# The first gather of the experts' tokens, ordered part by part and split around half of the first gate

## The chip, the core and the metric

The kernel runs on one core of a Trainium2 chip. Five engines work from instruction streams of their own and meet through semaphores: TensorE (PE, matrix products; its weight loads are listed apart as PEld), VectorE (DVE), ScalarE (ACT), GpSimd (POOL) and SyncE (SP), which here issues nearly all DMAs. The metric is the device time of one execution in microseconds (us), as the median of several runs.

## What is computed

One decoder block over 272 tokens of width 1024 (16 meta tokens and 256 real ones): a pooling mixer and a gated delta rule side by side, an output projection, and then a mixture of 32 experts in 4 groups. Only the last part matters here:

```
u = rmsnorm(h, norm_ffn_w)
p_grp, g_idx = top_k(softmax(u @ w_grp + b_grp), 1)            # one of 4 groups
w_e, e_idx   = top_k(softmax(expert logits of that group), 2)  # two of its 8 experts
for each expert e:                                             # 32 of them
    hdn = silu(u @ w_gate[e]) * (u @ w_up[e])                  # 1024 -> 512
    y  += (comb[:, e] * hdn) @ w_down[e]                       # 512 -> 1024
out = rmsnorm(h + y, norm_final_w)[:, 16:]
```

The weights of an expert are three arrays of 2 MiB in float32, 201 MB for all 32, and each is read once.

## The kernel before

**The experts' stage.** An expert computes at most 64 tokens (`SLOTS`). A matrix `hot` (token x slot, one or zero) picks them: the product of x, held as a rounded part `xhi` and a remainder `xlo` (both in the format of fast products), with `hot` gathers the tokens of four experts at once, transposed, 256 columns wide. The tokens come in two tiles of 128 (`TT` = 2, index t), the width 1024 in eight k tiles of 128 rows (`KT`), two of which make a *part* (`PARTS` = 4). A gathered part stands in a PSUM bank, from which a copy that multiplies by the norm's gain takes it to `xgT` (in the trace a piece of `bench`).

**The first gather** (`gather_first`, L2155 to L2184) has a bank for each part (`FIRST_BANK`, L2163): parts 0 to 3 in banks 5, 4, 7 and 6. It runs the products of `xhi` for parts 0 to 2, tile by tile, then those of `xlo` for parts 0 to 2, and then part 3 with both. ScalarE takes parts 0 and 2 to `xgT` (L1118, semaphore `xgT_side`), VectorE parts 1 and 3 (`bring`, L1723, semaphore `xgT`), all on `gathered`. VectorE makes `hot` (L1662) and then the remainders (`lows`, L1668): first the columns of parts 0 to 2 for both tiles, then those of part 3.

**Gate, up and down.** `gate_up` (L2218) multiplies the 64 slots of an expert by its gate and then its up weights, eight k tiles each, two products in a tile (two for each one in the trace, since these are float32). The first gate waits on `xgT_side` ahead of k tiles 0 and 4 and on `xgT` ahead of 2 and 6. It writes bank 5, where part 0 had stood. Behind it stand two products that count the tokens of the experts (`count_all`, L2110 and L2111), then up, then two parts of the next gather (L2142), then down (L2276).

**The stream of weights.** SyncE fills a ring of nine slots of 2 MiB and a spare half slot. Load n is array n % 3 (gate, up, down) of expert n // 3. Loads 9 to 18 come in two halves each (L743), shifted by half a slot: the first half of load 9 goes to the spare half, its second half into the first half of slot 0, the first half of load 10 into the second half of slot 0, and so on. The second half of load 9 is issued when gate 0 has read k tiles 0 to 3 (semaphore `half`), the first half of load 10 when gate 0 is done (`gate`), and so on with up and down. SyncE issues in this order and waits for each in turn.

**VectorE behind the first gather**: `bring(0, 1)`, `bring(0, 3)`, `weigh` (what the exponentials on ScalarE need), `weighed` (the weights of the two experts of each token, L1688 to L1694), `settle` (the largest count, L1699), and then `slots_of(1)`, which makes `hot` of the next four experts (L1710).

## Time and profile before

| | |
|---|---|
| median of 3 runs | 772.37 us (772.29 to 773.62) |
| profiled execution | 772.13 us |
| its span, first to last instruction | 770.4 us |
| PE busy | 750.6 us (97%) |
| DVE / ACT / POOL busy | 323.0 / 311.6 / 124.9 us |
| DMA | 240.56 MB, mean 312 GB/s |
| chain that ended last | PE 83%, DMA 11%, DVE 3%, issue 2%, ACT 1% |

Times in the rows are from the start of the span. The experts' stage begins at 318 and fills the rest. A time of an engine that waits is only a loss if what waits for that engine is late; so the profile is read by stage, and each wait by who comes last. Durations overlap on one engine (an instruction is listed until its result is written, the next starts before that), so what a piece occupies is read from the starts of two in a row.

### The profile page before, as it was taken

Reading aid. Unit: us, or ns where it says so; the run is one execution under the profiler, and the core shown is the slowest. Engines: PE = TensorE matmul, PEld = TensorE weight load, DVE = VectorE, ACT = ScalarE, POOL = GpSimd, SP = SyncE. Lnnn points to the kernel's source line nnn. Section 1 sums busy time; section 2 is a strip of 40 time slices with the busy share of each in tenths; the row PEclk is TensorE's granted clock in tenths of the full one; section 3 lists DMA queues with packets and bytes.
Section 4 is the critical chain, followed back from the end, with each engine's and each line's share of the span. In section 5 each row is a group of like instructions: output and inputs, shape, how many; then the busy total and the mean of one; then the engine's idle time right before and its main releaser. Section 6 shows DMA issues by size and latency. Waiting matters only on the chain.

```text
span 770.4 us, 16167 instructions
## 1 busy us (share of the span) xinstructions
PE 750.6 (97%) x6544; PEld 538.9 (70%) x6544; DVE 323.0 (42%) x795; ACT 311.6 (40%) x632; POOL 124.9 (16%) x209
## 2 busy tenths in 40 slices
PE   8999999999999999999999999999999999998995
PEld 8989989998999988755555555565555555455552
DVE  4895787678675855712211311221222113012112
ACT  6976678576684744712112121222112121111123
POOL 7473242225423640000000000000000000000000
PEclk9999999999999999999999999999999999999999
DMA  8537554554754479999999999999999999999993
GB/s 206 148 86 194 149 145 131 138 151 111 191 140 125 153 241 327 374 407 421 427 424 430 426 428 427 429 424 428 425 428 427 427 429 424 430 426 428 422 415 127
DMA packets 83265, 240.56 MB, mean 312 GB/s; under 512 B 7281, under 2 KB 65762, under 8 KB 69746
## 3 DMA queue, kind: packets, MB, share of 16 engines
q1 hardware_dynamic: 82882, 238.67, 81.4%
q8 instruction: 55, 0.90, 0.5%
q10 hardware_dynamic: 304, 0.79, 0.4%
q14 instruction: 24, 0.20, 0.1%
HBM read 238.40 MB, written 1.05 MB: 311 GB/s over the span
## 4 chain that ended last, share of the span: by engine, by line
PE 83%; DMA 11%; DVE 3%; issue 2%; ACT 1%; SPq 0%; DVEq 0%
PE banks L2218 24%; PE banks L1863 22%; PE banks L2276 12%; DMA ring<-in_expert_w_up_dram 10%; PE banks L2142 3%; PE banks L2231 3%; PE banks L2060 3%; PE banks L1983 1%; PE banks L1996 1%; PE banks L2252 1%; PE banks L2044 1%; PE banks L2000 1%; PE banks L1987 1%; DMA room<-in_w_in_dram 1%; PE banks L2021 1%
## 5 line engine op out<-in xcount | busy, mean ns | idle before, releaser
L2218 PE MATMUL banks<-ring,bench 128*64 128x256 f32 x2016 | 235.6, 388 | 5.1 <-DMA ring<-in_expert_w_up_dram 3.6
L2218 PEld LDWEIGHTS banks<-ring,bench 128*64 128x64 f32 x2016 | 144.5, 134 | 102.6 <-issue 19.5
L1863 PE MATMUL banks<-rounded 128*128 128x256 f32 (+2 forms) x1320 | 193.5, 293 | 0.4 <-DVE room L1481 0.4
L1863 PEld LDWEIGHTS banks<-rounded 128*128 128x128 f32 x1320 | 168.0, 188 | 3.7 <-issue 0.6
L1762 DVE TENSOR_TENSOR bench<-banks,bench 128x256 f32<-128x256 f32 x32 | 13.6, 424 | 254.3 <-PE banks L2218 182.7
L2276 PE MATMUL banks<-ring,bench 128*64 128x512 f32 x512 | 116.9, 598 | 0.3 <-ACT bench L1144 0.3
L1155 ACT ACTIVATE ysb<-banks 64x512 f32<-64x512 f32 x63 | 37.3, 592 | 150.3 <-PE banks L2276 149.5
L2276 PEld LDWEIGHTS banks<-ring,bench 128*64 128x64 f32 x512 | 33.9, 136 | 62.8 <-issue 60.2
L923 ACT ACTIVATE rounded<-room 128x1024 fp32r<-128x1024 f32 x64 | 67.4, 1054 | 22.1 <-PE banks L1863 15.0
L1144 ACT ACTIVATE bench<-banks 128x256 f32<-128x256 f32 x32 | 12.3, 385 | 142.8 <-PE banks L2252 142.8
L1381 DVE TENSOR_TENSOR rounded<-room,rounded 128x1024 fp32r<-128x1024 f32 x49 | 62.4, 1273 | 15.2 <-ACT rounded L923 14.2
L1250 POOL TENSOR_TENSOR rounded<-room,rounded 128x256 fp32r<-128x256 f32 x60 | 44.1, 767 | 60.7 <-ACT rounded L923 60.7
L1732 DVE SCALAR_TENSOR_TENSOR ylo<-ysb,bench,yhi 128x512 fp32r<-128x512 f32 x30 | 21.2, 749 | 64.6 <-ACT yhi L1162 64.6
L1432 DVE SCALAR_TENSOR_TENSOR desk<-banks,prmT,desk 128x271 f32<-128x271 f32 (+5 forms) x72 | 35.3, 490 | 4.6 <-ACT desk L933 2.5
L1139 ACT ACTIVATE bench<-banks 128x256 f32<-128x256 f32 x32 | 12.3, 384 | 57.1 <-PE banks L2218 57.1
L2142 PE MATMUL banks<-hot,xhi 128*128 128x256 f32 x112 | 34.6, 332 | 0.0
L1723 DVE TENSOR_TENSOR bench<-banks,gain 128x512 f32<-128x512 f32 x30 | 20.8, 692 | 20.8 <-PE banks L2142 18.7
L2142 PEld LDWEIGHTS banks<-hot,xhi 128*128 128x128 f32 x112 | 21.1, 188 | 11.2 <-issue 11.2
L2142 PE MATMUL banks<-hot,xlo 128*128 128x256 f32 x112 | 28.8, 280 | 0.0
L2231 PE MATMUL banks<-yhi,give 128*128 128x512 f32 x60 | 23.7, 396 | 0.0
L2231 PE MATMUL banks<-ylo,give 128*128 128x512 f32 x60 | 23.5, 391 | 0.0
L2142 PEld LDWEIGHTS banks<-hot,xlo 128*128 128x128 f32 x112 | 21.3, 191 | 0.2 <-issue 0.2
(317 smaller groups left out, 876.4 us busy)
## 6 DMA issues: line engine op xcount, KB each, us to landing
ring<-in_expert_w_down_dram SPq DMA_DIRECT2D x27, 2048.0 KB, 24.8
ring<-in_expert_w_up_dram SPq DMA_DIRECT2D x25, 2048.0 KB, 26.9
ring<-in_expert_w_gate_dram SPq DMA_DIRECT2D x24, 2048.0 KB, 25.9
room<-in_w_in_dram SPq DMA_DIRECT2D x56, 512.0 KB, 4.0
ring<-in_expert_w_gate_dram SPq DMA_DIRECT2D x10, 1024.0 KB, 9.8
ring<-in_expert_w_up_dram SPq DMA_DIRECT2D x8, 1024.0 KB, 10.4
ring<-in_expert_w_up_dram SPq DMA_DIRECT2D x12, 512.0 KB, 6.5
ring<-in_expert_w_down_dram SPq DMA_DIRECT2D x6, 1024.0 KB, 8.7
```

The lines of the kernel that those rows point to most:

```text
L923: nc.scalar.activation(whi[:, n % HI_SLOTS], win[:, n % WIN_SLOTS].rearrange("p k c -> p (k c)"), ACT.Copy).then_inc(S("whi"), 1)
L1155: nc.scalar.activation(ysb[g * SLOTS:(g + 1) * SLOTS, half * 512:(half + 1) * 512], pb[7][half * 64:half * 64 + SLOTS, :], ACT.Copy).then_ ...
L1250: ins = nc.gpsimd.tensor_tensor(wlo[:, lo_slot(n), cols], w[:, cols], whi[:, n % HI_SLOTS, cols].bitcast(F32), ALU.subtract)
L1381: V.tensor_tensor(wlo[:, lo_slot(n)], w, whi[:, n % HI_SLOTS].bitcast(F32), ALU.subtract).then_inc(S("wlo"), 1)
L1432: ins = V.scalar_tensor_tensor(acc[:, i, f + sh:L], p[:, 0:L - f - sh], prmT[:, tap * 24 + col:tap * 24 + col + 1], acc[:, i, f + sh:L], A ...
L1732: V.scalar_tensor_tensor(ylo[:, cols], ysb[:, cols], wslot[:, 0:1], yhi[:, cols].bitcast(F32), ALU.mult, ALU.subtract).then_inc(S("ylo"), 1)
L1863: ins = T.matmul(o, a, b[:, k, lo_at:L], start=(k == 0 and n == 0), stop=(k == KT - 1 and n == 2))
L2060: ins = T.matmul(pb[2 * i + half], a[:, i * P:(i + 1) * P], w[:, half * 512:(half + 1) * 512], start=(kk == 0 and first), stop=(kk == KT - ...
L2142: ins = T.matmul(pb[4][:, k * WIDE:(k + 1) * WIDE], x[:, t, ch:ch + P], hot[:, t, :], start=(t == 0 and x is xhi), stop=(t == TT - 1 and x ...
L2218: ins = T.matmul(pb[5 + c][half * 64:half * 64 + SLOTS, 0:256], xgT[:, q % ROOMS, kt, j * SLOTS:(j + 1) * SLOTS], ws[kt // 4][:, kt % 4, h ...
L2231: ins = T.matmul(pb[2 * t + half], give[:, t * P:(t + 1) * P], y[:, half * 512:(half + 1) * 512], start=False, stop=True, skip_group_check ...
L2276: ins = T.matmul(pb[7][half * 64:half * 64 + SLOTS, :], hT[:, j % 2, j // 2 * SLOTS:(j // 2 + 1) * SLOTS], ws[j // 2][:, j % 2, half * 512 ...
```

## The change

The first gather goes part by part, each with its remainders: parts 0 and 1 ahead of gate 0, then k tiles 0 to 3 of gate 0, then parts 2 and 3, then k tiles 4 to 7. VectorE makes the remainders in eight pieces of 256 columns in the same order, those of part 3 behind `bring(0, 1)`, and `weigh` stands ahead of `bring(0, 3)`. ScalarE's and SyncE's instructions stay as they are.

```diff
--- before.py
+++ after.py
@@ -1672,9 +1672,13 @@
             pick(1)
             first_slots(0)
             first_slots(1)
-            for cols in (slice(0, 3 * D // PARTS), slice(3 * D // PARTS, D)):
+            def part_lows(part):
+
                 for i in range(TT):
-                    lows(i, cols)
+                    lows(i, slice(part * D // PARTS, (part + 1) * D // PARTS))
+
+            for part in range(PARTS - 1):
+                part_lows(part)
 
             def weigh():
 
@@ -1744,8 +1748,9 @@
                 else:
                     dve.wait_ge(S("kept"), 1)
                     bring(0, 1)
+                    part_lows(PARTS - 1)
+                    weigh()
                     bring(0, 3)
-                    weigh()
                     weighed()
                     settle()
                 for e in range(EXPERTS):
@@ -2152,35 +2157,27 @@
                                        ident[:, n * 64:(n + 1) * 64], start=True, stop=True, skip_group_check=True)
                     ins.then_inc(S("gathered"), 1)
 
-                def gather_first():
-
-                    per = KT // PARTS
-
-                    def products(x, part, t):
-
-                        for k in range(per):
-                            ch = (part * per + k) * P
-                            ins = T.matmul(pb[FIRST_BANK[part]][:, k * WIDE:(k + 1) * WIDE], x[:, t, ch:ch + P], hot[:, t, :],
-                                           start=(k == 0 and t == 0 and x is xhi), stop=(t == TT - 1 and x is xlo), skip_group_check=True)
-                        return ins
-
-                    for t in range(TT):
-                        pe.wait_ge(S("hot"), t + 1)
-                        pe.wait_ge(S("xhi"), t + 1)
-                        for part in range(PARTS - 1):
+                per = KT // PARTS
+
+                def products(x, part, t):
+
+                    for k in range(per):
+                        ch = (part * per + k) * P
+                        ins = T.matmul(pb[FIRST_BANK[part]][:, k * WIDE:(k + 1) * WIDE], x[:, t, ch:ch + P], hot[:, t, :],
+                                       start=(k == 0 and t == 0 and x is xhi), stop=(t == TT - 1 and x is xlo), skip_group_check=True)
+                    return ins
+
+                def gather_parts(some):
+
+                    for part in some:
+                        for t in range(TT):
+                            pe.wait_ge(S("hot"), t + 1)
+                            pe.wait_ge(S("xhi"), t + 1)
                             products(xhi, part, t)
-                    for t in range(TT):
-                        pe.wait_ge(S("xlo"), t + 1)
-                        for part in range(PARTS - 1):
+                        for t in range(TT):
+                            pe.wait_ge(S("xlo"), TT * part + t + 1)
                             ins = products(xlo, part, t)
-                            if t == TT - 1:
-                                ins.then_inc(S("gathered"), 1)
-                    for t in range(TT):
-                        products(xhi, PARTS - 1, t)
-                    for t in range(TT):
-                        pe.wait_ge(S("xlo"), TT + t + 1)
-                        ins = products(xlo, PARTS - 1, t)
-                    ins.then_inc(S("gathered"), 1)
+                        ins.then_inc(S("gathered"), 1)
 
                 def landed(e, c):
 
@@ -2208,6 +2205,8 @@
                             pe.wait_ge(S("give"), pairs + i)
                     ws = [half_at(3 * e + c, n, again).rearrange("p (k q h j) -> p k h q j", k=KT // 2, h=2, j=2) for n in range(2)]
                     for kt in range(KT):
+                        if first and c == 0 and kt == KT // 2:
+                            gather_parts(range(PARTS // 2, PARTS))
                         if first and c == 0 and kt % 4 == 0:
                             pe.wait_ge(S("xgT_side"), kt // 4 * 2 + 2)
                         if first and c == 0 and kt % 4 == 2:
@@ -2284,7 +2283,7 @@
                         for k in range(KT // PARTS):
                             gather(0, part, k)
                 else:
-                    gather_first()
+                    gather_parts(range(PARTS // 2))
                 for e in range(EXPERTS):
                     q, j, i, g = e // 4, e % 4, e // 2, e % 2
                     gate_up(e, 0, "gate")
```

On TensorE, at the start of the experts' stage, before. The rows give the line, the operation, out<-in and how many in a row; L2163 is the first gather, L2218 gate 0 and then up 0, L2110 and L2111 the counting:

```order
L2106 MATMUL banks<-ticks,give 128x32
L2163 MATMUL banks<-hot,xhi 128x256 x12
L2163 MATMUL banks<-hot,xlo 128x256 x12
L2163 MATMUL banks<-hot,xhi 128x256 x4
L2163 MATMUL banks<-hot,xlo 128x256 x4
L2218 MATMUL banks<-ring,bench 64x256 x16
L2110 MATMUL banks<-ticks,give 128x32
L2111 MATMUL banks<-ticks,give 128x32
L2218 MATMUL banks<-ring,bench 64x256 x16
```

The same place now; the gather is L2166 and the gate L2217:

```order
L2111 MATMUL banks<-ticks,give 128x32
L2166 MATMUL banks<-hot,xhi 128x256 x4
L2166 MATMUL banks<-hot,xlo 128x256 x4
L2166 MATMUL banks<-hot,xhi 128x256 x4
L2166 MATMUL banks<-hot,xlo 128x256 x4
L2217 MATMUL banks<-ring,bench 64x256 x8
L2166 MATMUL banks<-hot,xhi 128x256 x4
L2166 MATMUL banks<-hot,xlo 128x256 x4
L2166 MATMUL banks<-hot,xhi 128x256 x4
L2166 MATMUL banks<-hot,xlo 128x256 x4
L2217 MATMUL banks<-ring,bench 64x256 x8
L2115 MATMUL banks<-ticks,give 128x32
```

Gate 0 is cut in two, and the sixteen products of parts 2 and 3 stand in the cut.

On VectorE, from the second `hot` on, before; L1668 are the remainders, L1723 the brings, L1681 and L1683 `weigh`, and from L1688 on `weighed`:

```order
L1662 TENSOR_TENSOR hot<-iota_c,bench 128x256
L1668 SCALAR_TENSOR_TENSOR xlo<-late,rs,xhi 128x768 x2
L1668 SCALAR_TENSOR_TENSOR xlo<-late,rs,xhi 128x256 x2
L1723 TENSOR_TENSOR bench<-banks,gain 128x512 x2
L1681 TENSOR_SCALAR rs<-bench 128x1 x2
L1683 TENSOR_TENSOR rs<-bench 128x1 x2
L1688 RECIPROCAL rs<-rs 128x1 x2
```

The same place now, with L1727 the brings and L1685 and L1687 `weigh`:

```order
L1662 TENSOR_TENSOR hot<-iota_c,bench 128x256
L1668 SCALAR_TENSOR_TENSOR xlo<-late,rs,xhi 128x256 x6
L1727 TENSOR_TENSOR bench<-banks,gain 128x512
L1668 SCALAR_TENSOR_TENSOR xlo<-late,rs,xhi 128x256 x2
L1685 TENSOR_SCALAR rs<-bench 128x1 x2
L1687 TENSOR_TENSOR rs<-bench 128x1 x2
L1727 TENSOR_TENSOR bench<-banks,gain 128x512
L1692 RECIPROCAL rs<-rs 128x1 x2
```

The two brings are apart now: one behind six pieces of the remainders, the other behind the last two and `weigh`, and everything from L1692 on behind it.

## Rows read from the trace of the kernel before

**Rows 1.** Windows: each engine's busy us (x instructions), PE clock, DMA share, GB/s.

```profile
345.00:445.00 100.00, 100.00 (x705) 57.38 (x705) 21.71 (x51) 20.01 (x39) 0.00 (x0) 1.00 1.01 426
```

**Rows 2.** Chain that ended last: start us, us, what; gate and up of two experts, then loads.

```profile
430.15 7.26 PE banks L2218 x64
...
456.87 7.26 PE banks L2218 x64
...
611.91 36.88 DMA ring<-in_expert_w_up_dram
```

**Rows 3.** Windows around the gap in the DMA engines' work; columns as in Rows 1.

```profile
324.50:327.00 2.50, 2.50 (x24) 1.46 (x22) 1.95 (x14) 1.90 (x5) 0.00 (x0) 1.00 0.64 164
...
329.00:333.00 4.00, 4.00 (x30) 2.39 (x28) 2.01 (x6) 0.39 (x1) 0.00 (x0) 1.00 1.00 354
```

**Rows 4.** Timeline of SyncE's DMA issues: start us, us, line, operation, out<-in, count.

```profile
315.37 0.33 SPq L743 DMA_DIRECT2D spare<-in_expert_w_gate_dram  x1
324.84 0.33 SPq L743 DMA_DIRECT2D ring<-in_expert_w_gate_dram  x1
326.65 2.62 SPq L743 DMA_DIRECT2D ring<-in_expert_w_up_dram  x2
330.75 3.78 SPq L743 DMA_DIRECT2D ring<-in_expert_w_down_dram  x2
```

**Rows 5.** DMA issues, windows 324.5:325.5 and 326.3:327.5: kind, count, KB each, us to landing.

```profile
ring<-in_expert_w_gate_dram SPq DMA_DIRECT2D x1, 1024.0 KB, 4.8
...
ring<-in_expert_w_up_dram SPq DMA_DIRECT2D x1, 1024.0 KB, 6.4
```

**Rows 6.** Timeline of PE, 316 to 331; [idle before <-releaser].

```profile
318.47 1.70 PE L2163 MATMUL banks<-hot,xhi 128*128 128x256 f32 x12 [0.31 <-DVE hot L1662]
320.00 1.88 PE L2163 MATMUL banks<-hot,xlo 128*128 128x256 f32 x12
321.72 0.64 PE L2163 MATMUL banks<-hot,xhi 128*128 128x256 f32 x4
...
322.76 3.85 PE L2218 MATMUL banks<-ring,bench 128*64 128x256 f32 x32
326.54 0.28 PE L2110 MATMUL banks<-ticks,give 128*128 128x32 f32 x1
...
330.64 0.39 PE L2142 MATMUL banks<-hot,xhi 128*128 128x256 f32 x1
```

**Rows 7.** Timeline of DVE, windows of 314 to 334, some cut between two remainders.

```profile
318.57 0.43 DVE L1662 TENSOR_TENSOR hot<-iota_c,bench 128x256 fp32r<-128x256 f32 x1
...
318.91 1.01 DVE L1668 SCALAR_TENSOR_TENSOR xlo<-late,rs,xhi 128x768 fp32r<-128x768 f32 x1
...
319.85 1.41 DVE L1668 SCALAR_TENSOR_TENSOR xlo<-late,rs,xhi 128x768 fp32r<-128x768 f32 x2
...
320.77 0.87 DVE L1668 SCALAR_TENSOR_TENSOR xlo<-late,rs,xhi 128x256 fp32r<-128x256 f32 x2
...
321.17 0.48 DVE L1668 SCALAR_TENSOR_TENSOR xlo<-late,rs,xhi 128x256 fp32r<-128x256 f32 x1
...
321.76 0.69 DVE L1723 TENSOR_TENSOR bench<-banks,gain 128x512 f32<-128x512 f32 x1
...
324.80 0.23 DVE L1688 RECIPROCAL rs<-rs 128x1 f32<-128x1 f32 x2 [0.85 <-ACT rs L1125]
...
327.34 0.75 DVE L1710 TENSOR_TENSOR hot<-iota_c,bench 128x256 fp32r<-128x256 f32 x2
```

**Rows 8.** Timeline of PEld (weight loads), 314 to 334.

```profile
320.91 0.77 PEld L2163 LDWEIGHTS banks<-hot,xlo 128*128 128x128 f32 x6 [0.16 <-DVE xlo L1668]
```

**Rows 9.** Timeline of ACT around 321.5: the copies of parts 0 and 2.

```profile
321.51 0.48 ACT L1118 ACTIVATE bench<-banks,gain 128x256 f32<-128x256 f32 x1 [2.11 <-PE banks L2163]
...
321.88 1.20 ACT L1118 ACTIVATE bench<-banks,gain 128x256 f32<-128x256 f32 x3
```

## The prediction

> **What bounds the kernel now.** I read the profile from its end backwards. First the stretch 345 to 445: the 16 DMA engines are busy all the time, at 426 GB/s [rows 1], and TensorE is busy too, so the reader has to ask which of the two is ahead. The chain of waits answers. Two experts take TensorE 456.87 - 430.15 = 26.72 us [rows 2] and use six loads of 2.097 MB, 12.58 MB; the stream needs 12.58 MB / 426 GB/s = 29.5 us for them. TensorE is thus faster by 2.8 us in each pair, frees ring slots sooner than they can be filled, and the queue of loads grows, until a load issued at 611.91 takes 36.88 us to land and TensorE starts to wait for weights [rows 2]. The end of the kernel is therefore set by the stream of weights. A delay of TensorE at 320 us costs nothing by itself (over the ten pairs up to 611.91 TensorE gains some 28 us on the stream); it costs what it leaves the DMA engines **without work**.
>
> That makes one hole the thing to look at. From 324.5 to 327.0 the DMA engines are busy 0.64 of the time and move 164 GB/s [rows 3]: idle 0.36 x 2.5 = 0.90 us, and short of 426 GB/s by 0.66 MB, 1.54 us of the stream. It is there because SyncE may issue the next half load only once gate 0 has read the first half of its weights (issue at 324.84), and the one behind it once gate 0 is done (326.65); the load before these was issued at 315.37 [rows 4]. A half load is 1.049 MB, 2.46 us of the stream. The one of 324.84 landed after 4.8 us [rows 5], so 4.8 - 2.46 = 2.34 us pass besides the transfer.
>
> **The part that changes, before.** TensorE starts the first gather at 318.47, gate 0 at 322.76, and is done with gate 0 at 326.54, where the counting products stand [rows 6]. These are 32 products of the gather and 32 of the gate (two in the trace for each one in the code). 16 of the gate take (326.54 - 322.76) / 2 = 1.89 us, 0.118 us each, and at that pace 64 make 7.55 us; the stretch took 8.07, so the stalls in it are 0.52 us.
>
> **What the change does to VectorE.** No product is added. The remainders are eight instructions of 256 columns for two of 768 and two of 256. From the starts 318.91 and 319.85 a 768 piece occupies VectorE 0.94 us, from 320.77 and 321.17 a 256 piece 0.40 us [rows 7]. Six pieces ahead of the first bring are 2.40 us against 2 x 0.94 + 2 x 0.40 = 2.68 us before it; after that two follow it. They end 0.48 us after their start [rows 7]: at 319.39, 319.79, 320.19, 320.59, 320.99, 321.39.
>
> The Trainium skill, "VectorE: DVE Perf Modes", section "The TRN2 errata — SBUF-src ops pay a fixed extra latency per instruction", speaks against this split: the fixed cost is paid by each piece, and it wants 512 elements or more. The starts here bear out a fixed part of 0.40 - 256 x (0.54 / 512) = 0.13 us, 0.52 us for four more instructions; by the rule alone the change would lose that much if VectorE were the limit, and by the rows it is hidden, since the first piece is ready sooner.
>
> **TensorE through the first half.** It now starts with two products of part 0 for tile 0, 318.47 to 318.71. Tile 1's `hot` is ready at 318.57 + 0.43 = 319.00 [rows 7]; six products covered this wait, two do not. With 0.06 us from VectorE's end to TensorE (318.91 + 1.01 + 0.06 = 319.98, close to the 320.00 of the first remainder product), it goes on at 319.06 to 319.30, waits for the remainder of 319.39, runs 319.45 to 319.69, waits for that of 319.79, runs 319.85 to 320.09. Part 1 needs no waits that matter: 320.09 to 321.04 (its second remainder is ready at 320.65, and wanted at 320.80).
>
> Now gate 0 must wait for part 0's copy, which was hidden before behind the products of part 3. The pair that closed part 0 began at 320.91 [rows 8] and ScalarE started the copy at 321.51 [rows 9], 0.60 us later. So ScalarE starts at 319.85 + 0.60 = 320.45; its second copy started 0.37 us after the first and takes 0.48 [rows 9], ready at 321.30. Gate 0 starts at 321.36, a **new stall** of 0.32 us. Its k tiles 2 and 3 need VectorE's bring of part 1: that pair begins at 320.80, so the bring starts at 321.40, takes 0.69 [rows 7], and is ready at 322.09, where TensorE wants it at 321.36 + 0.94 = 322.30. Hidden, with 0.2 us to spare. The first half of gate 0 ends at 321.36 + 1.89 = 323.25.
>
> **Through the second half.** Parts 2 and 3 run 323.25 to 325.14; their remainders are long there. Part 2's closing pair begins at 323.96, ScalarE copies from 324.56, ready at 325.41, and TensorE goes on at 325.47: a **second stall** of 0.33 us. VectorE's bring of part 3 starts at 324.90 + 0.60 = 325.50 and is ready at 326.19, wanted at 326.41. Gate 0 ends at 325.47 + 1.89 = 327.36. Against 326.54 TensorE is **0.8 us later**. The rest of VectorE's queue moves with it: the weights of the experts (from 324.80 before) wait now behind the bring, start near 326.3, and the `hot` of 327.34 comes near 329.6 [rows 7]; the gather that wants it is at 330.64 + 0.8 [rows 6]. Hidden, by 1.5 us or more; if it were not, TensorE would stall by the difference.
>
> **What the stream gets.** The half of slot 0 is freed at 323.25 instead of 322.76 + 1.89 = 324.65; with the 0.19 us to the issue of 324.84, SyncE issues at 323.44, **1.40 us earlier**. The next issue is at 326.65 + 0.8 = 327.45, **later**, and so are all behind it. By landings: before 324.84 + 4.8 = 329.64, and the next could land by the later of 329.64 + 2.46 = 332.10 and 326.65 + 4.8 = 331.45, thus 332.10. After: 323.44 + 4.8 = 328.24, and the next by the later of 330.70 and 327.45 + 4.8 = 332.25. The hole is not closed, it is moved behind the early half load. The stream stands **0.15 us later** than before. The following half loads, 0.8 us later too, have slack: the one issued near 334.20 (the second of the two from 330.75 to 334.53 [rows 4]) could land at 335.0 + 4.8 = 339.8 and the stream is at 332.25 + 3 x 2.46 = 339.63, another 0.17 us at most. I take 0.15: the measured landing 326.65 + 6.4 = 333.05 [rows 5] is 0.95 behind the 332.10 of this sum, so that the queue really was fuller than the sum has it. The same row bounds the gain: with 0.95 us more in the queue before the later load the stream could come out 0.9 us earlier, the idle of the hole; the other end is the whole delay of TensorE, +0.8.
>
> The profiled execution took 772.13 us, its span 770.4. With +0.15 it is 772.28; it stands 0.24 under the median of 772.37, so I carry the difference to the median: **772.5 us**.
>
> **The rivals.**
> *TensorE's delay counts in full* (the queue is not the limit where I think): 772.37 + 0.8 = 773.2. For it: TensorE is 100 us of 100 busy [rows 1]. Against: the wait of 36.88 us for a load [rows 2].
> *The hole is closed*: the early half load fills it and the later one finds the queue still busy. 0.9 us of idle come back, 771.4. For it: the landing of 333.05; against: one half load holds 2.46 us, and 327.45 - 323.44 is 4.0.
> *The short pieces cost more*, the rule above: were pieces issued every 0.48 us, their full duration, the sixth would end at 321.79, bring 1 would be ready at 322.48, TensorE wanted it at 322.30; gate 0 ends 0.2 to 0.4 us later still, 772.8. The starts of 320.77 and 321.17 speak against it. The page named above is where it comes from.
> *Slower by over 0.2%*: TensorE stops before every pair of k tiles of gate 0, because each hand-over (product, copy, product: 0.60 + 0.85 us) is exposed in full. That is 4 x 1.45 = 5.8 less the 2 x 1.9 of cover that products of other parts give, some 2.0 us more, so 2.8 in all, and the hole takes it one for one beyond the 0.65 us of slack (332.10 - 331.45) : 774.5. It decides from a delay of 2.2 us on. The brings have 0.2 us to spare twice, which is what speaks for it; that all four are late by so much is unlikely.
> *Faster by over 0.2%*: all of the 1.54 us and the shortfall at 329 to 333 (426 - 354 GB/s over 4 us, 0.68 us [rows 3]) come back: 770.2.
>
> **How the numbers follow.** 0.2% is 1.54 us, about what a measurement can tell here from no change. Forecast 0.55; full delay 0.15; hole closed 0.17; short pieces 0.04; slower 0.06; faster 0.03. The first four lie within 0.2%: 0.91. For the range: down to the closed hole, 771.4; up past the full delay, 773.2, to 772.5 + 1.25 = 773.8, since one of the three runs shown lies 1.25 us above the median. Left outside: the two last rivals and little more.
>
> **What would show each step.** In the new profile: gate 0 starting near 321.4 with a short idle before it, counted from 318.47 of the first product; a second idle of 0.3 before its second half; the counting products near 327.4; the issues of SyncE at 323.4 and 327.5; and the low share of the DMA engines cut in two, one piece near 325 and one near 328.5. The forecast is wrong if the counting products come before 327.0 or after 328.5, if ScalarE or VectorE starts its copies more than 0.2 us off the times above, or if the DMA engines show one hole or none.

## The result: 1.4 us slower, and the profile after

| | before | after |
|---|---|---|
| median of 22 runs | 772.47 us | 773.99 us |
| ratio | | 1.0018 (95% interval 1.0012 to 1.0024) |
| profiled execution | 772.13 us, span 770.4 | 775.07 us, span 773.3 |
| first product of the gather | 318.47 | 319.70 (318.42 in a second trace) |

The change costs 1.4 us (0.9 to 1.9). The profiled executions are 2.9 apart; that the first product comes 1.2 us later in the first trace after is the spread of single executions, as the second trace of the same kernel shows. All that follows is therefore counted **from the first product of the gather**, which I call zero. Three executions of the experiments, which took 830 to 3821 us, are slow ones and count in no ratio.

TensorE after, from zero = 319.70 (against [rows 6]; L2166 is the gather, L2217 the gate and up, L2115 the counting):

```profile
319.70 1.09 PE L2166 MATMUL banks<-hot,xhi 128*128 128x256 f32 x4 [0.31 <-DVE hot L1662]
320.69 0.90 PE L2166 MATMUL banks<-hot,xlo 128*128 128x256 f32 x4
321.42 0.64 PE L2166 MATMUL banks<-hot,xhi 128*128 128x256 f32 x4
321.90 0.63 PE L2166 MATMUL banks<-hot,xlo 128*128 128x256 f32 x4
322.67 2.03 PE L2217 MATMUL banks<-ring,bench 128*64 128x256 f32 x16
324.63 0.73 PE L2166 MATMUL banks<-hot,xhi 128*128 128x256 f32 x4
325.20 0.62 PE L2166 MATMUL banks<-hot,xlo 128*128 128x256 f32 x4
325.65 0.64 PE L2166 MATMUL banks<-hot,xhi 128*128 128x256 f32 x4
326.13 0.63 PE L2166 MATMUL banks<-hot,xlo 128*128 128x256 f32 x4
326.75 2.03 PE L2217 MATMUL banks<-ring,bench 128*64 128x256 f32 x16
328.71 0.28 PE L2115 MATMUL banks<-ticks,give 128*128 128x32 f32 x1
```

Gate 0 starts at 322.67 - 319.70 = 2.97, its second half at 7.05, and the counting stands at 9.01, where it stood at 8.07 before. TensorE is 0.94 us later. ScalarE's two pairs of copies, each with the wait in front of it (against [rows 9]):

```profile
321.69 0.84 ACT L1118 ACTIVATE bench<-banks,gain 128x256 f32<-128x256 f32 x2 [1.04 <-PE banks L2166]
325.86 0.84 ACT L1118 ACTIVATE bench<-banks,gain 128x256 f32<-128x256 f32 x2 [3.33 <-PE banks L2166]
```

VectorE; the brings are L1727, the remainders L1668, and L1714 is the `hot` of the next four experts (against [rows 7]):

```profile
319.81 0.43 DVE L1662 TENSOR_TENSOR hot<-iota_c,bench 128x256 fp32r<-128x256 f32 x1
320.15 2.46 DVE L1668 SCALAR_TENSOR_TENSOR xlo<-late,rs,xhi 128x256 fp32r<-128x256 f32 x6
322.64 0.69 DVE L1727 TENSOR_TENSOR bench<-banks,gain 128x512 f32<-128x512 f32 x1
323.25 0.87 DVE L1668 SCALAR_TENSOR_TENSOR xlo<-late,rs,xhi 128x256 fp32r<-128x256 f32 x2
...
326.80 0.69 DVE L1727 TENSOR_TENSOR bench<-banks,gain 128x512 f32<-128x512 f32 x1 [2.29 <-PE banks L2166]
327.47 0.22 DVE L1692 RECIPROCAL rs<-rs 128x1 f32<-128x1 f32 x2
...
329.96 0.76 DVE L1714 TENSOR_TENSOR hot<-iota_c,bench 128x256 fp32r<-128x256 f32 x2
```

SyncE's issues and landings (against [rows 4, 5]). The last of these lines is the load issued at 336.36, the second half of load 11:

```profile
324.73 0.33 SPq L743 DMA_DIRECT2D ring<-in_expert_w_gate_dram  x1
328.82 2.62 SPq L743 DMA_DIRECT2D ring<-in_expert_w_up_dram  x2
...
ring<-in_expert_w_gate_dram SPq DMA_DIRECT2D x1, 1024.0 KB, 5.7
...
ring<-in_expert_w_up_dram SPq DMA_DIRECT2D x1, 1024.0 KB, 5.2
...
ring<-in_expert_w_down_dram SPq DMA_DIRECT2D x1, 1024.0 KB, 8.0
```

The same load in the kernel before, issued at 334.20 (the prediction names it):

```profile
ring<-in_expert_w_down_dram SPq DMA_DIRECT2D x1, 1024.0 KB, 6.4
```

The second half of load 9 goes out at 5.03 (before 6.37), the first half of load 10 at 9.12 (before 8.18). And the stream, from 5 to 14, from 14 to 24 and from 24 to 34 us after zero, last number GB/s, the one before it the DMA engines' share. Before:

```profile
323.47:332.47 9.00, 9.00 (x74) 5.59 (x72) 4.94 (x29) 2.91 (x9) 0.00 (x0) 1.00 0.90 320
332.47:342.47 10.00, 10.00 (x76) 5.21 (x74) 0.48 (x1) 1.57 (x3) 0.00 (x0) 1.00 1.00 419
342.47:352.47 10.00, 10.00 (x62) 5.32 (x60) 2.14 (x5) 2.75 (x5) 0.00 (x0) 1.00 1.01 421
```

After; the two last lines are single stretches, from 9.5 to 11.5 and from 19 to 23:

```profile
324.70:333.70 9.00, 9.00 (x74) 6.12 (x73) 4.33 (x22) 3.24 (x10) 0.00 (x0) 1.00 0.92 324
333.70:343.70 10.00, 10.00 (x74) 5.54 (x74) 1.31 (x4) 1.96 (x4) 0.00 (x0) 1.00 0.91 351
343.70:353.70 10.00, 10.00 (x64) 5.28 (x60) 1.78 (x4) 1.80 (x4) 0.00 (x0) 1.00 1.02 428
329.20:331.20 2.00, 2.00 (x20) 1.23 (x20) 1.45 (x6) 0.02 (x1) 0.00 (x0) 1.00 0.74 164
338.70:342.70 4.00, 4.00 (x40) 2.59 (x36) 0.00 (x0) 0.98 (x2) 0.00 (x0) 1.00 0.84 299
```

Up to 14 us the changed kernel is no worse, 324 against 320 GB/s: the hole stands, later (164 GB/s from 9.5 to 11.5). By the packets' records it is even ahead: 14 us after zero it had moved 60.02 MB in both of its traces, the kernel before 59.91 and 59.79, a mean of 0.17 MB less or 0.4 us of the stream. The loss comes **after the hole**, where the kernel before moves 419 GB/s and the changed one 351: 68 GB/s over 10 us are 0.68 MB, 1.6 us of the stream. Worst is 19 to 23 us after zero, 299 GB/s. The second half of load 11 shows it too: it landed 8.0 us after its issue, 24.6 us after zero, where it took 6.4 us and landed at 22.1 before. From 24 us on both are at full rate (428 and 421 GB/s). What is lost there is not made up: the stream has no idle time left to make it up in, and the load issued at 614.11 waits 37 us in the queue, as that of [rows 2] did:

```profile
614.11 37.22 DMA ring<-in_expert_w_up_dram
```

The trace has a record of every packet. I give three things from these records, each worked out by going through them: the number of packets of 8 KiB that took over 0.55 us (the usual ones take 0.31; below, "slow packets") and start between 14 and 24 us after zero; the time from zero at which 150 MB of the kernel's transfers had landed, "the stream" below; and the end of the last instruction from zero.

```
kernel        gate 0 done   slow packets 14 to 24    150 MB landed     end
before             8.07               1                  226.08       451.94
before_again       8.07               0                  226.21       452.41
after              9.01              17                  227.29       453.64
after_again        9.01              27                  227.24       453.72
after_mid          9.03               9                  227.00       453.23
late_half          9.00               0                  228.06       454.12
delay_8            9.03               5                  227.01       453.16
delay_16           9.99              12                  227.90       454.07
parts_only         9.94               6                  227.80       454.36
covered            8.47              13                  226.66       453.07
sp_later           8.06               1                  226.06       452.29
one_late           8.06              14                  226.65       453.12
no_stall           7.76               4                  225.69       451.53
quarters           7.76               1                  225.73       452.17
```

Two traces of one kernel agree within 0.13 us in the stream and 0.5 in the end, so the stream is the sharper measure. Against the mean of the two before (226.15) the changed kernel's stream is 1.1 us late, its end 1.5 (452.18), its time 1.4. Times of the experiments are ratios to runs of the kernel before on the same chip; their intervals are 0.7 to 0.9 us to either side, so small effects are read in the traces, each a single execution unless said.

### The profile page after: what moved, and what is told of

Read it like the earlier page. It is cut to its first block, busy times and chain, and to the rows that moved or that the text cites. A ratio compares the mean times of both kernels' runs of the same rounds, so it can differ in the third digit from the quotient of the medians.

```text
span 773.3 us, 16177 instructions
## 1 busy us (share of the span) xinstructions
PE 751.8 (97%) x6544; PEld 539.3 (70%) x6544; DVE 322.7 (42%) x799; ACT 311.7 (40%) x632; POOL 126.2 (16%) x209
## 3 DMA queue, kind: packets, MB, share of 16 engines
HBM read 238.40 MB, written 1.05 MB: 310 GB/s over the span
## 4 chain that ended last, share of the span: by engine, by line
PE 81%; DMA 11%; issue 3%; POOL 2%; DVE 2%; ACT 1%; POOLq 0%; DVEq 0%; ACTq 0%
PE banks L2217 24%; PE banks L1868 21%; PE banks L2275 12%; DMA ring<-in_expert_w_up_dram 10%; PE banks L2147 3%; PE banks L2230 3%; PE banks L2065 3%; PE banks L2001 1%; PE banks L1988 1%; PE banks L2251 1%; PE banks L2049 1%; PE banks L2005 1%; PE banks L1992 1%; PE banks L2026 1%; PE banks L2010 1%
## 5 line engine op out<-in xcount | busy, mean ns | idle before, releaser
L2217 PE MATMUL banks<-ring,bench 128*64 128x256 f32 x2016 | 235.8, 388 | 5.9 <-DMA ring<-in_expert_w_up_dram 3.6
L2217 PEld LDWEIGHTS banks<-ring,bench 128*64 128x64 f32 x2016 | 144.5, 134 | 103.4 <-issue 20.5
L1736 DVE SCALAR_TENSOR_TENSOR ylo<-ysb,bench,yhi 128x512 fp32r<-128x512 f32 x30 | 21.2, 750 | 64.9 <-ACT yhi L1162 64.9
L1727 DVE TENSOR_TENSOR bench<-banks,gain 128x512 f32<-128x512 f32 x30 | 20.8, 692 | 22.5 <-PE banks L2147 18.7
```

Source lines behind the costliest of these rows:

```text
L1736: V.scalar_tensor_tensor(ylo[:, cols], ysb[:, cols], wslot[:, 0:1], yhi[:, cols].bitcast(F32), ALU.mult, ALU.subtract).then_inc(S("ylo"), 1)
L2217: ins = T.matmul(pb[5 + c][half * 64:half * 64 + SLOTS, 0:256], xgT[:, q % ROOMS, kt, j * SLOTS:(j + 1) * SLOTS], ws[kt // 4][:, kt % 4, h ...
```

## The experiments

**The kernels themselves once more.** No edit, for the spread of a trace.

> The changed kernel once more, beside the others on one chip and for a second trace. If the 1.2 us by which its first product came later than before in the first trace (319.70 against 318.47) belongs to the kernel, it is seen again; if it is the spread of single executions, the first product stands near 318.5 and only what follows it is slower: gate 0 done at 9.0, the first load that TensorE waits for 1.3 us later than before, both from the first product, and the time up by 1.0 to 1.5 us.

Measured: ratio 1.0020 (1.0011 to 1.0029), 1.5 us; first product at 318.42, so "lost upstream" falls; gate 0 done at 9.01 again, and again the loss stands between 14 and 24 (here the DMA engines' share is 1.00 and 27 packets are slow; in the first trace it is 0.91 with 17 slow packets, for the same loss):

```profile
323.42:332.42 9.00, 9.00 (x73) 6.15 (x73) 4.33 (x22) 3.24 (x10) 0.00 (x0) 1.00 0.92 324
332.42:342.42 10.00, 10.00 (x74) 5.34 (x74) 1.30 (x4) 1.95 (x4) 0.00 (x0) 1.00 1.00 356
```

> The kernel before once more, for a second trace to measure against. All theories alike: gate 0 done 8.07 us after the first product, and the stream where it was in the first trace, within 0.2 us; how far the first product itself moves is the spread of single executions.

Measured: first product at 317.98, gate 0 done at 8.07, stream 0.13 us from the first trace, and no loss behind 14:

```profile
322.98:331.98 9.00, 9.00 (x74) 5.70 (x72) 4.95 (x29) 2.91 (x9) 0.00 (x0) 1.00 0.89 309
331.98:341.98 10.00, 10.00 (x76) 5.45 (x74) 0.48 (x1) 1.57 (x3) 0.00 (x0) 1.00 1.00 422
```

**TensorE later, nothing moved.** In the kernel before, products more ahead of part 3:

```diff
+                    for _ in range(8):
+                        T.matmul(pb[FIRST_BANK[PARTS - 1]][:, 0:WIDE], xhi[:, 0, 0:P], hot[:, 0, :], start=True, stop=True, ...)
                     for t in range(TT):
                         products(xhi, PARTS - 1, t)
```

> The kernel before with eight products more (256 columns, into part 3's bank, whose first real product clears it) ahead of part 3: gate 0 ends 8 x 0.118 = 0.94 us later, as much as in the changed kernel, and nothing is moved or released earlier. Theory 'lateness' (the end of gate 0 and all issues behind it being 0.9 us later is the whole cause): slower than before by 1.2 to 1.6 us, like the change (1.4). Rival 'slack' (the sum on record: the queue has 0.65 us to spare before the load behind gate 0): slower by 0.3 us, so that the change's loss comes from the early half load and what it does to the queue. Rival 'upstream' (the time is lost ahead of the first gather, where the changed program only lies elsewhere in memory): no effect of the products beyond 0.3 us.

> As the kernel with eight products more, but sixteen: gate 0 ends 1.89 us later than before. Theory 'lateness in full': the stream stands 1.8 to 1.9 us behind the kernel before, measured from the first product (0.96 for eight), and the time is up by about the same. Rival 'slack': 1.89 - 0.65 = 1.2. Rival 'fixed price' (the stream loses 1 us once the queue is thin, whatever the delay): 1.0.

Measured: with eight, 1.0007 (0.9999 to 1.0016), the stream 0.86 us late, the end 1.0; with sixteen, 1.0026 (1.0016 to 1.0035), 2.0 us, the stream 1.75, the end 1.9. TensorE was late by 0.96 and 1.92. The delay goes to the stream nearly one for one, so there is no fixed price. In time, eight products cost 0.5 us (-0.1 to 1.2), less than the 1.2 to 1.6 that 'lateness' was written down with; sixteen cost what it said. The rival 'slack' is not tested by these two, though it was set against them: they delay the second half of load 9 as well, and to that issue the sum on record gives no slack (332.10 comes from its landing), so that the sum says 0.96 and 1.92 here, as 'lateness' does. The slack was meant for the issue behind it, which sp_later below delays alone. But the loss lies elsewhere than in the changed kernel. With eight:

```profile
323.55:332.55 9.00, 9.00 (x76) 5.60 (x74) 4.69 (x26) 2.52 (x8) 0.00 (x0) 1.00 0.78 280
332.55:342.55 10.00, 10.00 (x74) 5.54 (x74) 1.32 (x4) 1.96 (x4) 0.00 (x0) 1.00 1.00 413
```

The first stretch has it (280 against 320 GB/s over 9 us, 0.36 MB, 0.84 us), the second hardly any. Here the half load that ends the hole, the second half of load 9, is itself later (7.32 for 6.37), and the hole grows by that. In the changed kernel it is earlier, and the loss stands behind the hole.

**Part by part without the cut in gate 0.** The changed kernel with all four parts ahead of gate 0:

```diff
-                        if first and c == 0 and kt == KT // 2:
-                            gather_parts(range(PARTS // 2, PARTS))
...
-                    gather_parts(range(PARTS // 2))
+                    gather_parts(range(PARTS))
```

> One part of the change alone: part by part with its remainders, all four parts ahead of gate 0, no cut in the gate. Stalls of TensorE: 0.3 for the second hot, 0.3 for the first two remainders, none for copies (part 0's is ready 1.3 us before it is wanted), so gate 0 ends 0.1 to 0.2 us later than before. 'Lateness': slower than before by 0 to 0.3 us. 'Slack': no difference. Rival that the pieces on VectorE are the cost: near the 1.4 us of the change.

A miss: gate 0 was done at 9.94, 1.87 us later than before, not 0.1 to 0.2. Here VectorE sets TensorE's pace: each pair of remainders' products (0.24 us) waits for a piece that takes 0.40 us, and part 3's pieces stand behind the bring of part 1.

```profile
318.20 1.09 PE L2166 MATMUL banks<-hot,xhi 128*128 128x256 f32 x4 [0.31 <-DVE hot L1662]
319.18 0.90 PE L2166 MATMUL banks<-hot,xlo 128*128 128x256 f32 x4
319.92 0.88 PE L2166 MATMUL banks<-hot,xhi 128*128 128x256 f32 x4
320.59 1.05 PE L2166 MATMUL banks<-hot,xlo 128*128 128x256 f32 x4
321.44 1.05 PE L2166 MATMUL banks<-hot,xhi 128*128 128x256 f32 x4
322.30 1.05 PE L2166 MATMUL banks<-hot,xlo 128*128 128x256 f32 x4
323.15 0.81 PE L2166 MATMUL banks<-hot,xhi 128*128 128x256 f32 x4
323.80 0.63 PE L2166 MATMUL banks<-hot,xlo 128*128 128x256 f32 x4
324.36 3.85 PE L2215 MATMUL banks<-ring,bench 128*64 128x256 f32 x32
```

The stream is 1.65 us late, the end 2.2. The timed runs say 1.0006 (0.9996 to 1.0015), 0.5 us and at most 1.2. These don't fit together. The profiled execution took 774.37 us, 1.05 above the median of its twelve (773.32), so it may not be typical; a second trace, which would settle it, was not taken. What holds is that the cut in gate 0 saves the changed kernel 0.9 us of TensorE's time against this.

**The early half load taken away.** The changed kernel; SyncE waits for the end of gate 0 ahead of the second half of load 9:

```diff
-                        sp.wait_ge(S("half"), n - RING + 1)
+                        sp.wait_ge(S("gate" if n == RING else "half"), n - RING + 1)
```

> The changed kernel, but the second half of load 9 is issued only when gate 0 is done, with the first half of load 10 right behind. What the early release gives: if the half load that comes 4 us earlier is work for the DMA engines that they would otherwise not have, this kernel is slower than the changed one by up to 2.46 us, and by about 1.9 by the landings' sum (328.8 + 4.8 = 333.6 and 336.1, against 334.0 measured for the same load). If the stream regains it, no difference. By 'lateness' and 'slack' alike about +1.9 against the changed kernel, +3.3 against before; a rival by which the early half load is what hurts says faster than the changed kernel.

Measured: 1.0017 (1.0008 to 1.0026), 1.3 us, like the changed kernel; stream 1.9 us late (0.8 behind the changed one), end 1.9. The 1.9 us that I expected against the changed kernel are 0.8 in the stream, and in the timed runs nothing that can be told. Where the loss went:

```profile
323.31:332.31 9.00, 9.00 (x73) 6.14 (x73) 4.34 (x22) 3.24 (x10) 0.00 (x0) 1.00 0.61 228
332.31:342.31 10.00, 10.00 (x74) 5.52 (x74) 1.29 (x4) 1.96 (x4) 0.00 (x0) 1.00 1.01 428
```

The hole is larger (228 GB/s), but behind it the stream runs at 428 GB/s without one slow packet. Two half loads went out together (9.11 and 9.48), and each of the next four came to its first packet 4.0 to 5.0 us after its issue, so the queue stayed filled.

**The early half load less early.** The changed kernel, with one wait more, for ScalarE's copy of part 2:

```diff
+                        if n == RING:
+                            sp.wait_ge(S("xgT_side"), KT // PARTS * 2)
                         sp.wait_ge(S("half"), n - RING + 1)
```

> The changed kernel, with one wait more on SyncE: the second half of load 9 is issued when ScalarE has copied part 2, near 7.0 us after the first product (changed 5.03, before 6.37, gate 0 done 9.0). TensorE is as in the changed kernel. Theory 'lead': a load that comes to the DMA engines less than some 2.8 us after its issue pays a start of up to 1 us again, and the early half load makes the queue thin behind it, so that the two next ones pay; issued 2 us later there is one hole and one start. Then the stream stands, against the first product, 0.9 to 1.0 us behind the kernel before, where the changed kernel stands 1.3 behind: 0.3 to 0.4 us better for issuing later. Rival 'slack and landings' (the sum on record): issuing later can only cost, 0 to 0.5 us.

Measured: issue at 7.04 instead of 5.03, TensorE as in the changed kernel (9.03). The stream is 0.27 us **earlier** than in the changed kernel's two traces, the end 0.45; the timed runs can't tell them apart (1.0019, 1.0008 to 1.0029, against 1.0020 on the same chip). The loss behind 14 us is a third of what it was, the hole is larger:

```profile
323.07:332.07 9.00, 9.00 (x73) 6.11 (x73) 4.30 (x22) 3.24 (x10) 0.00 (x0) 1.00 0.82 294
332.07:342.07 10.00, 10.00 (x74) 5.36 (x74) 1.32 (x4) 1.95 (x4) 0.00 (x0) 1.00 0.98 397
```

So the two microseconds by which the half load is early are worth nothing, or less. This was expected by the theory of a thin queue, though the difference is small.

One comparison of traces helps to sort the causes. delay_8, after_mid and the changed kernel issue everything from load 10 on at the same times (9.12 to 9.15, 11.41 to 11.44, 13.22 to 13.25, 16.66 to 16.69), 0.94 to 0.97 us later than before. They differ in the second half of load 9: 7.32, 7.04 and 5.03. Their streams are late by 0.86, 0.85 and 1.12 us. Moving the half load by 0.28 us, from 7.04 to 7.32, moves nothing, so the 0.86 us seem to come with the later issues that all four traces share; the early half load adds 0.26 us and takes nothing away. That is a reading of the traces and not an experiment: in delay_8 and after_mid the half load is also 0.7 to 1.0 us later than before.

**SyncE alone later, first issue.** The kernel before, TensorE untouched; the first half of load 10 waits for VectorE's largest count:

```diff
+                        if n == RING + 1:
+                            sp.wait_ge(S("most"), 1)
                         load_half(sp, n, 0)
```

> The kernel before, in which SyncE alone is later: the first half of load 10 is issued when VectorE has the largest count (near 9.0 us after the first product) instead of when gate 0 is done (8.18). TensorE ends gate 0 at 8.07 as before and all later issues keep their times (10.47, 12.28). Theory 'the first issue behind gate 0 sets the stream': the stream stands 0.7 to 0.9 us behind the kernel before, and so does the end. Theory 'all issues together' (TensorE's lateness counts since every issue behind gate 0 is late): well under half of that, since the later ones find room. The sum on record (slack of 0.65 us): 0.1 to 0.2.

Measured: issued at 9.03 instead of 8.18, and no effect: 1.0000 (0.9991 to 1.0009), stream 0.1 us earlier, end 0.1 later. The theory that this issue sets the stream falls; the sum on record had the slack of this one issue right.

**SyncE alone later, one issue behind the hole.** The kernel before; the second half of load 11 goes out when down 0 is done, not at its middle:

```diff
+                        if n == RING + 2:
+                            used_up(n - RING)
                         sp.wait_ge(S("half"), n - RING + 1)
```

> The kernel before, in which SyncE alone is later, and with one issue only: the second half of load 11 goes out when down 0 is done (near 17.4 us after the first product) instead of at its middle (15.73). TensorE and all other issues stay (12.28 before it, 17.44 behind it, which becomes 17.8). In the kernel before the DMA engines finish the half load ahead of it near 18.8, 3.1 us after its issue; here that is 1.4 us, less than in the changed kernel (1.9 to 2.1). Theory 'thin queue': each engine starts it with a packet of 1 to 1.6 us instead of 0.31, as in the changed kernel, and the next load too: between 14 and 24 us after the first product the DMA engines move 360 to 395 GB/s instead of 419, and the stream stands 0.6 to 1.3 us behind. Rival 'issued in time is enough' (first packets were seen 0.95 us after an issue, 17.44 + 0.95 = 18.4, before 18.8): 410 GB/s or more, and no shift over 0.2 us; then the changed kernel's loss has to come from the products' copies and the code around them, not from the queue.

Measured: 1.0013 (1.0002 to 1.0024), 1.0 us slower; the stream 0.50 late, the end 0.95. TensorE was done with gate 0 at 8.06.

```profile
323.17:332.17 9.00, 9.00 (x74) 5.69 (x72) 4.93 (x29) 2.91 (x9) 0.00 (x0) 1.00 0.90 319
332.17:342.17 10.00, 10.00 (x76) 5.21 (x74) 0.47 (x1) 1.57 (x3) 0.00 (x0) 1.00 0.99 391
```

The first stretch is as before (319), the second falls from 419 to 391 GB/s, 0.66 us. By the packets' records the DMA engines finished the half load ahead between 18.5 and 19.3, and the late one had gone out at 17.44; the first packets were seen 0.95 to 0.97 us behind an issue in other places (in the kernel before, issue 6.37, packets from 7.34), so by that it was there in time. But ten packets that start between 18.5 and 19.6 took 0.56 to 1.18 us instead of 0.31. In the kernel before, the same half load goes out at 15.73 and none of its packets is slow. The rival "issued in time is enough" falls, and the loss is made with TensorE's gate 0, its copies and its order untouched. It came out at the small end of what was expected (391 of 360 to 395 GB/s; the stream at 0.50, under the 0.6).

In the changed kernel that half load goes out at 16.66, in both traces, and the one behind it at 18.38. The slow packets of the first trace from 18 us on, start from zero and duration in us:

```
18.85 0.60   19.15 1.45   19.45 0.73   20.05 0.96   21.00 1.47   21.20 1.53   21.37 1.10
21.54 1.02   21.80 0.64   22.05 0.74   22.63 0.59
```

This one half load can be followed through all traces. A half load is 128 packets; counting them in order of start gives the start of its first packet and the time until the next half load's first, 2.46 us at the full rate (the engines are somewhat out of step, so the count is good to a few tenths). Against the time from its issue to its first packet, which says how much other work was in the queue:

```
kernel         issue to first packet    its 128 packets
one_late               1.22                   3.26
after                  2.12                   3.66
after_again            2.16                   3.54
after_mid              2.55                   2.91
covered                2.60                   3.02
parts_only             2.75                   2.55
delay_16               2.88                   2.58
delay_8                2.93                   2.45
no_stall               2.95                   2.49
before                 2.99                   2.45
sp_later               3.12                   2.45
before_again           3.19                   2.46
late_half              3.97                   2.45
```

With 2.6 us or less the half load lost 0.45 to 1.2 us, with 2.75 and 2.88 us 0.1, with 2.93 or more nothing. That this time alone decides is not shown: the second half of load 10 had only 1.9 us in both traces of the changed kernel and ran at full pace (2.5 us).

**All copies covered, gate cut.** The changed kernel, but whole products of parts 0 to 2 first, their remainders, the whole products of part 3, half of gate 0, the remainders of part 3, the other half:

```diff
-                    gather_parts(range(PARTS // 2))
+                    whole_products(range(PARTS - 1))
+                    low_products(range(PARTS - 1))
+                    whole_products([PARTS - 1])
...
-                            gather_parts(range(PARTS // 2, PARTS))
+                            low_products([PARTS - 1])
```

> A version that should beat both: whole products of parts 0 to 2 for both tiles, their remainders part by part, the whole products of part 3, then the first half of gate 0, the remainders' products of part 3, the second half. Every copy has products of another part beside it. TensorE: 64 products of 0.118 us and 0 to 0.2 us of stalls, so gate 0 ends 7.6 to 7.8 us after the first product (before 8.07, changed 9.01), and its first half ends at 5.2 (before 6.17, changed 4.9). The next two issues are 1.0 and 0.3 us earlier than before. 'Lateness' and the landings' sum: faster than before by 0.7 to 1.0 us. A rival by which the cut of the gate itself costs (an early half load in a nearly empty queue): as slow as before or slower.

A miss: 1.0012 (1.0002 to 1.0021), 0.9 us slower than before. Gate 0 was done at 8.47, not 7.7. From the first of TensorE's twelve remainders' products of parts 0 to 2 to the next product passed 1.78 us, though they are 1.42 us of work, since six pieces of 0.40 us on VectorE again set their pace; another 0.2 us were lost at the cut, and the rest in pieces of 0.1. The half load went out at 5.94, its follower at 8.58, and the second half of load 11 at 16.12:

```profile
323.56:332.56 9.00, 9.00 (x73) 5.55 (x68) 4.81 (x24) 2.46 (x8) 0.00 (x0) 1.00 0.88 319
332.56:342.56 10.00, 10.00 (x76) 5.37 (x76) 0.77 (x2) 1.66 (x4) 0.00 (x0) 1.00 1.00 392
```

319 GB/s in the first stretch, no better than before for all its earlier issue, and 392 in the second. TensorE was 0.4 us late, the stream 0.5. The rival, as slow as before or slower, came true, but its reason (the cut of the gate) is not shown by it, since TensorE was late as well.

**No stall, no cut.** The kernel before, with the whole products of all four parts first, and VectorE's remainders in pieces of 256, 512 and 256 columns for each tile:

```diff
+                    for t in range(TT):
+                        products(xhi, PARTS - 1, t)
+                    for n, some in enumerate(([0], range(1, PARTS - 1), [PARTS - 1])):
+                        for t in range(TT):
+                            pe.wait_ge(S("xlo"), TT * n + t + 1)
+                            for part in some:
+                                ins = products(xlo, part, t)
```

> The kernel before with its order on TensorE and VectorE changed so that nothing waits, and gate 0 uncut: whole products of all four parts, then the remainders' products of part 0, of parts 1 and 2, of part 3; VectorE makes part 0's remainders first. The 64 products take 7.55 us plus 0 to 0.1, so gate 0 ends 7.6 us after the first product instead of 8.07. 'Lateness in full', read the other way: the stream and the end 0.4 to 0.5 us earlier than before, near what can be told. 'Slack' or 'fixed price': nothing gained, 0.

Measured: gate 0 done at 7.76, the stream 0.45 us and the end 0.65 earlier than in the mean of the two traces before; the timed runs can't tell it: 1.0000 (0.9991 to 1.0009), 772.33 us against 772.5. The same kernel, with one half load cut once more:

> The kernel in which no copy and no remainder is waited for (gate 0 done at 7.76), and in it the first half of load 10 is cut in two: its first quarter is issued when gate 0 has read k tiles 4 and 5, near 6.9 us after the first product, its second at 7.9. If the first issue behind gate 0 sets the stream: up to 0.9 us earlier than the same kernel without the cut, which makes it 1.2 us earlier than the kernel before, and faster by about as much. If each load started on a nearly empty queue pays again, as the changed kernel's early half did: 0 to 0.3 us, and the time within 0.1% of before.

```diff
+                        if n == RING + 1:
+                            for s in range(2):
+                                cols = slice(s * CHUNK // 4, (s + 1) * CHUNK // 4)
+                                if s:
+                                    used_up(0)
+                                else:
+                                    sp.wait_ge(S("quarter"), 1)
+                                sp.dma_start(half_at(n, 0, False)[:, cols], up_v[n // 3][:, cols]).then_inc(...)
```

Measured: the quarter went out at 6.96, the stream stood where it did without it (225.73 and 225.69), the time 1.0004 (0.9995 to 1.0014). An issue that is earlier by itself gives nothing here either. (The diff shows SyncE's part alone; the order on TensorE and VectorE is that of the kernel above.)

## Why the prediction was wrong

The recorded forecast was 772.5 us and no difference to be told, its range ended at 773.8; the measured 773.99 lies 0.2 us outside, and the change is slower by more than its interval. By its steps (times from zero):

- **What bounds the kernel: right.** The stream of weights sets the end; a delay near 320 us is absorbed by TensorE's lead and counts only through the stream. one_late and the chain show it: one_late delays no product of TensorE's first gate and costs the end 0.95 us.
- **TensorE's steps: right, a little small in size.** Expected start of gate 0, second half and end, from zero: 2.89, 7.00, 8.89. Measured 2.97, 7.05, 9.01. Delay 0.94 instead of the 0.8 on record. ScalarE's copies were expected at 1.98 and 6.09, and started at 1.99 and 6.16. Both new stalls are there. VectorE's weights started at 7.77, as expected (7.8). The `hot` behind them came at 10.26, not at 11.1: in [rows 7] it stands 2.54 us behind the weights, and 326.3 + 2.54 is 328.8, not the 329.6 of the text. The gather that wants it stood at 332.81, which is 13.1 from zero, so it cost nothing.
- **The issues: right.** Expected 4.97 and 8.98, measured 5.03 and 9.12.
- **The hole: right in kind.** It was moved, not closed. By 14 us the stream stood 0.4 us ahead of the kernel before, where the sum had it 0.15 behind. sp_later shows that the slack of the issue behind the hole was real.
- **"The following half loads have slack, another 0.17 us at most": this is the step that failed.** The sum let a load follow the one before it without loss as long as it had been issued 4.8 us ahead of its own landing. For the load that it names, issued near 334.20 before, it had the stream at 339.63, 21.2 from zero. That load landed at 24.6 and 24.1 in the two traces of the changed kernel, and at 22.1 and 22.4 in those of the kernel before. In the changed kernel the half load ahead had been issued 1.34 us earlier and the next issues came 0.94 later, so that less work stood in the queue when each was made (2.1 us instead of 3.0 ahead of the one named). Behind the hole, 17 and 27 packets took 0.56 to 1.73 us in place of 0.31, in the first trace the engines also idled, and 1.6 us of the stream were lost between 14 and 24 us. one_late makes such a loss by a single late issue (0.5 us in the stream), and late_half shows it gone where the queue stays filled. The term was 0.17 and measured 1.6; less the 0.4 gained at the hole, the stream is 1.1 to 1.2 us late.
- **A sign that was read the wrong way.** The prediction took the late landing of [rows 5] (333.05, 0.95 behind the sum's 332.10) for a fuller queue, and left the slack as it was. The packets of the same trace say otherwise: twelve that start between 10.6 and 13.5 us after zero took 0.57 to 1.24 us. The kernel before lost time there in the same way.
- **The price at the end.** The end is 0.3 to 0.45 us later again than the stream at 150 MB (1.5 against 1.1). In all the kernels that are slower the difference in the end is larger than in the stream, by 0.0 to 0.5, and the two traces before differ by 0.5 in the end. I have no experiment on that.
- **The rivals.** "TensorE's delay counts in full", 773.2, was nearest, with a chance of 0.15. Its reason (the queue is not the limit) is wrong, but its price comes near: delay_8 and after_mid, with the same later issues, lose 0.86 us of the stream, and the changed kernel 1.12. The rule of the Trainium skill on short pieces ("VectorE: DVE Perf Modes", section "The TRN2 errata — SBUF-src ops pay a fixed extra latency per instruction") stood behind a rival of 0.04. It did not decide the change, whose gate 0 ended 0.12 us off the forecast with the pieces counted at 0.40 us each. But short pieces did hold up two of my own variants, parts_only and covered: six pieces of 0.40 us in a row are slower than the products that want them.

The changed order does two things: it frees the half slot 1.3 us earlier, which in the end is worth nothing, and it ends gate 0 0.94 us later, which costs. Not tested is the kernel before with all issues behind the first half of load 10 late and nothing else; it would say how much of the loss they make together. No version here beats the kernel before by more than can be measured; no_stall is the best in the traces.

## What to carry to other kernels

Where a stream of loads bounds the end, ask of every reordering how full the queue is when each of the next loads gets its turn, and not only whether the load is there in time. An earlier first issue that drains before the next can be made trades one hole for a thin queue. Before an engine's order is changed for the sake of an earlier release, look whether the releases behind it come later.

## What the runs showed of the hardware

- A half load (8 packets of 8 KiB for each of the 16 DMA engines) that starts on an idle queue: the first packets 0.95 to 0.97 us behind the issue (6.37 to 7.34 in the kernel before; late_half 9.11 to 10.07), 14 and 16 of them take 0.57 to 1.24 us, the others 0.31.
- The same slow packets are seen where a load was issued before its turn came but little other work stood in the queue. For the second half of load 11, 2.6 us or less from its issue to its first packet went with a loss of 0.45 us or more, 2.93 us or more with none (the table under one_late). The second half of load 10 had 1.9 us in the changed kernel and lost nothing, so a single lead time does not sort all cases. What makes the packets slow, and whether the engine transfers or waits in that time, the runs don't show.
- Two half loads issued 0.37 us apart behind a long hole (late_half): 16 slow packets at the start of the first, none from 14 to 24 us, and 428 GB/s there.
